# Gate and up projection of an FFN: six more chunk pairs by seven products, one product of two taken over by GpSimd, and a reordered opening

## The reference, cut to what matters

```python
xn = rms_norm(x, ffn_norm_g[l])                    # x * rsqrt(mean(x^2) + eps) * g
gate, up = jnp.split(xn @ w_gate_up[l], 2, axis=-1)  # 1024 -> 2 * 2816
x = x + (jax.nn.silu(gate) * up) @ w_down[l]
```

## Time and profile before

| what | us |
|---|---|
| median of three runs | 1330.39 |
| profiled execution | 1330.17 |
| its span | 1328.5 |
| PE busy | 1303.2 (98%) |
| DVE busy | 806.3 (61%) |
| ACT busy | 575.9 (43%) |
| POOL busy | 465.6 (35%) |

### The profile page before, as it was taken

The page is one execution under the profiler, slowest core; times in us unless marked ns, Lnnn a source line. Parts: engine busy times, 40 slices in busy tenths (PEclk is TensorE's granted clock), DMA queues, the critical chain, the costliest instruction groups (busy, mean ns, idle before and its releaser), DMA issues.

```text
span 1328.5 us, 17433 instructions
## 1 busy us (share of the span) xinstructions
PE 1303.2 (98%) x6598; PEld 1088.7 (82%) x6598; DVE 806.3 (61%) x1245; ACT 575.9 (43%) x996; POOL 465.6 (35%) x210
## 2 busy tenths in 40 slices
PE   8999999999999999999999999999969999999998
PEld 6888888887878888888888888897758999998886
DVE  7998727233383366665534655578796777764443
ACT  5224333223242565666633345676443434433223
POOL 2455444444444443344444342343250000014441
PEclk9999999999999999999999999999989999999999
DMA  4233333334622422324333363433213333222321
GB/s 162 93 95 119 111 94 96 95 94 144 223 87 72 142 79 64 96 66 189 122 101 96 103 194 102 128 113 127 79 39 120 98 117 105 96 95 96 109 90 72
DMA packets 43260, 143.54 MB, mean 108 GB/s; under 512 B 6033, under 2 KB 6033, under 8 KB 42417
## 3 DMA queue, kind: packets, MB, share of 16 engines
q1 hardware_dynamic: 39376, 129.88, 30.8%
q10 hardware_dynamic: 3808, 12.64, 2.6%
HBM read 121.46 MB, written 10.49 MB: 99 GB/s over the span
## 4 chain that ended last, share of the span: by engine, by line
PE 92%; DVE 4%; ACT 2%; POOL 1%; DMA 1%; issue 1%; SPq 0%; DVEq 0%; ACTq 0%
PE bank L1875 29%; PE bank L1877 29%; PE bank L1876 29%; PE bank L2045 2%; POOL w_lo L618 1%; PE bank L2034 1%; PE bank L2035 1%; DVE xs L1684 1%; PE bank L1899 1%; ACT w_hi L686 0%; DMA x<-x_in 0%; DVE pool_sqsum L1185 0%; DVE xs L1690 0%; ACT pool_xg L712 0%; PE bank L2190 0%
## 5 line engine op out<-in xcount | busy, mean ns | idle before, releaser
L618 POOL TENSOR_TENSOR w_lo<-raw,w_hi 128x1024 fp32r<-128x1024 f32 (+1 forms) x148 | 371.2, 2511 | 567.3 <-ACT w_hi L686 567.2
L686 ACT ACTIVATE w_hi<-raw 128x1024 fp32r<-128x1024 f32 x149 | 156.2, 1054 | 230.6 <-PE bank L1877 181.8
L663 POOL TENSOR_TENSOR w_lo<-raw,w_hi 128x1024 fp32r<-128x1024 f32 x22 | 53.7, 2443 | 253.7 <-ACT w_hi L1090 253.7
L1875 PE MATMUL bank<-y_hi,w_hi 128*128 128x512 f32 x256 | 101.5, 396 | 0.0
L1876 PE MATMUL bank<-y_lo,w_hi 128*128 128x512 f32 x256 | 101.2, 396 | 0.0
L1877 PE MATMUL bank<-y_hi,w_lo 128*128 128x512 f32 x256 | 101.2, 395 | 0.0
L1875 PE MATMUL bank<-pool_xg,w_hi 128*128 128x512 f32 x248 | 98.4, 397 | 0.0
L1876 PE MATMUL bank<-pool_xg,w_hi 128*128 128x512 f32 x248 | 98.1, 396 | 0.0
L1877 PE MATMUL bank<-pool_xg,w_lo 128*128 128x512 f32 x248 | 98.1, 395 | 0.0
L1841 DVE TENSOR_TENSOR act<-acts,act 128x512 fp32r<-128x512 f32 x22 | 55.2, 2515 | 58.1 <-ACT act L1096 58.1
L1200 DVE TENSOR_TENSOR x<-bank,x 128x512 f32<-128x512 f32 x16 | 11.1, 692 | 118.4 <-PE bank L1877 115.3
(11 more groups left out here) (418 smaller groups left out, 3614.8 us busy)
## 6 DMA issues: line engine op xcount, KB each, us to landing
raw<-stream SPq DMA_DIRECT2D x187, 512.0 KB, 3.5
raw_x<-stream SPq DMA_DIRECT2D x18, 512.0 KB, 4.3
spill<-x ACTq DMA_DIRECT2D x2, 2048.0 KB, 7.3
xg_spill<-mla_xg ACTq DMA_DIRECT2D x2, 2048.0 KB, 11.9
rope_q<-turned_hl SPq DMA_DIRECT2D x64, 64.0 KB, 2.2
zx<-xg_spill SPq DMA_DIRECT2D x2, 1536.0 KB, 9.6
stacked<-fq SPq DMA_DIRECT2D x24, 128.0 KB
stacked<-fk SPq DMA_DIRECT2D x24, 128.0 KB
```

Source lines behind the costliest of these rows:

```text
L618: pool.tensor_tensor(w_lo[:, j % RING, 0:width], raw[:, j % RAW, 0:width], plain(w_hi[:, j % RING, 0:width]), ALU.subtract).then_inc(tile_ ...
L663: pool.tensor_tensor(w_lo[:, s, 0:D], raw[:, d % RAW, 0:D], plain(w_hi[:, s, 0:D]), ALU.subtract).then_inc(tile_lo, 1)
L686: act.activation(w_hi[:, t % RING, 0:width], raw[:, t % RAW, 0:width], ACT.Copy).then_inc(tile_hi, 1)
L1875: pe.matmul(target, a_hi, b_hi, start=start, stop=False)
```

## The change

Five edits, all in the FFN.

1. `PLAN` makes all 18 pairs from 4 to 21 "S".
2. gate*up of these pairs (`finish`, DVE) is removed; POOL makes it, in a loop of 18 instructions that stands behind its last front tile and ahead of its first down tile.
3. ACT multiplies x by the norm weights into xs (8 instructions ahead of the norm's root), and DVE multiplies by `inv` in 4 instructions of 128 x 1024 in place of 8 of 128 x 512.
4. ACT's splits of front tiles 4, 6 and 7 move ahead of the root, of three of the `scaled_high` and of `front_silu(1)`; DVE's `front_evacuate(1)` and `front_gate(1)` move behind the first two and three differences.
5. The sixth product (a22) goes to the first half of bank 0 in place of the second half of bank 1, and waits for one combining addition in place of four; the seventh waits for three.

```diff
-PLAN = "N" * FRONT + "SSN" * 6
+PLAN = "N" * FRONT + "S" * 18
...
             low_tiles(FIRST_OPERAND, first=TILE["mix"] + 24)
+            pool.wait_ge(act_ready, FRONT)
+            for p in range(FRONT, FC):
+                pool.wait_ge(gate_silu, p + 1)
+                pool.wait_ge(combined, COMBINED * (SEVENS.index(p) + 1))
+                pool.tensor_tensor(acts[:, p, :], acts[:, p, :], gated[:, p % 2, :], ALU.mult).then_inc(act_ready, 1)
             pool.wait_ge(tile_lo, DOWN)
...
             split_tile("ffn_up", 0, 0)
+            for k in range(DC):
+                act.activation(xs[:, k, :], x[:, k, :], ACT.Copy, scale=col("ffn_norm", k)).then_inc(n.xg_hi, 1)
+            split_tile("ffn_up", 0, 1)
             norm_root(norm["ffn"])
-            split_tile("ffn_up", 0, 1)
             front_silu(0)
             split_tile("ffn_up", 0, 2)
-            for i in range(DC // 2):
+            scaled_high(0)
+            split_tile("ffn_up", 0, 3)
+            for i in range(1, DC // 2):
                 scaled_high(i)
+            split_tile("ffn_up", 0, 4)
             front_silu(1)
-            split_tile("ffn_up", 0, 3)
-            split_tile("ffn_up", 0, 4)
...
-            def scaled(k):
-
-                dve.scalar_tensor_tensor(xs[:, k, :], x[:, k, :], col("ffn_norm", k), inv[:], ALU.mult, ALU.mult).then_inc(n.x_ready, 1)
+            def scaled(i):
+
+                c = xs[:, 2 * i:2 * i + 2, :]
+                dve.wait_ge(n.xg_hi, n.chunks + DC + 2 * i + 2)
+                dve.tensor_tensor(c, c, inv[:].unsqueeze(1).to_broadcast([P, 2, S]), ALU.mult).then_inc(n.x_ready, 1)
...
-            def finish(p):
-
-                dve.wait_ge(gate_silu, p + 1)
-                up = acts[:, p, :] if PLAN[p] == "S" else pair_banks(p)[1][:]
-                dve.tensor_tensor(acts[:, p, :], up, gated[:, p % 2, :], ALU.mult).then_inc(act_ready, 1)
...
             front_evacuate(0)
-            for c in range(DC):
-                scaled(c)
+            for i in range(DC // 2):
+                scaled(i)
             front_gate(0)
             for i in range(DC // 2):
                 scaled_low(i)
-            front_evacuate(1)
             dve.wait_ge(n.xg_lo, n.chunks + DC + DC // 2)
...
             dve.tensor_tensor(b12, b22, b12, ALU.subtract).then_inc(n.x_ready, 1)
-            front_gate(1)
+            front_evacuate(1)
...
             t_low(0)
+            front_gate(1)
...
                 if p == FRONT:
                     front_gate(p - 1)
-                else:
-                    finish(p - 1)
...
-                pe.wait_ge(combined, COMBINED * i + 4)
-                half_product(banks[1][:, second], p, "a22", *t_split("t4"), True, True)
+                pe.wait_ge(combined, COMBINED * i + 1)
+                half_product(banks[0][:, first], p, "a22", *t_split("t4"), True, True)
+                pe.wait_ge(combined, COMBINED * i + 3)
                 half_product(banks[2][:, second], p, "s4", *scaled_part(1, 1), True, True)
```

More of the change, by code:

```diff
@@ L1044, in scaled_high @@
             def scaled_high(i):
-                act.wait_ge(n.x_ready, DC + 2 * i + 2)
+                act.wait_ge(n.x_ready, DC + i + 1)
                 act.activation(xs_hi[:, 2 * i:2 * i + 2, :], xs[:, 2 * i:2 * i + 2, :], ACT.Copy).then_inc(n.xg_hi, 1)
             def t_high(i):
-                act.wait_ge(n.x_ready, 2 * DC + i + 1)
+                act.wait_ge(n.x_ready, DC + DC // 2 + i + 1)
                 source = xs[:, CHUNKS[(0, 0, 1, 1)[i]], TOKENS[(0, 1, 1, 0)[i]]]
@@ L1680, in front_gate @@
                 dve.tensor_tensor(acts[:, p, :], acts[:, p, :], front_gated[:, p % 2, :], ALU.mult).then_inc(act_ready, 1)
-            def scaled(k):
-                dve.scalar_tensor_tensor(xs[:, k, :], x[:, k, :], col("ffn_norm", k), inv[:], ALU.mult, ALU.mult).then_inc(n.x_ready, 1)
+            def scaled(i):
+                c = xs[:, 2 * i:2 * i + 2, :]
+                dve.wait_ge(n.xg_hi, n.chunks + DC + 2 * i + 2)
+                dve.tensor_tensor(c, c, inv[:].unsqueeze(1).to_broadcast([P, 2, S]), ALU.mult).then_inc(n.x_ready, 1)
             def scaled_low(i):
                 c = slice(2 * i, 2 * i + 2)
-                dve.wait_ge(n.xg_hi, n.chunks + DC + i + 1)
+                dve.wait_ge(n.xg_hi, n.chunks + 2 * DC + i + 1)
                 dve.tensor_tensor(xs_lo[:, c, :], xs[:, c, :], plain(xs_hi[:, c, :]), ALU.subtract).then_inc(n.xg_lo, 1)
@@ L1694, in t_low @@
             def t_low(i):
-                dve.wait_ge(n.xg_hi, n.chunks + DC + DC // 2 + i + 1)
+                dve.wait_ge(n.xg_hi, n.chunks + 2 * DC + DC // 2 + i + 1)
                 dve.tensor_tensor(t_lo[:, i], (b11, b12, b22, b21)[i], plain(t_hi[:, i]), ALU.subtract).then_inc(n.xg_lo, 1)
@@ L1752, in combine_up @@
             def combine_up(p):
-                combine(p, "a22", acts[:, p, TOKENS[0]], pair_banks(p)[1][:, TOKENS[1]], u3_sum)
+                combine(p, "a22", acts[:, p, TOKENS[0]], pair_banks(p)[0][:, TOKENS[0]], u3_sum)
             def combine_gate(p):
                 combine(p, "s4", gated[:, p % 2, TOKENS[1]], pair_banks(p)[2][:, TOKENS[1]], v_sum)
+            T_READY = DC + DC // 2
             front_evacuate(0)
-            for c in range(DC):
-                scaled(c)
+            for i in range(DC // 2):
+                scaled(i)
             front_gate(0)
@@ L1765, in _ @@
                 scaled_low(i)
-            front_evacuate(1)
             dve.wait_ge(n.xg_lo, n.chunks + DC + DC // 2)
-            dve.wait_ge(n.x_ready, 2 * DC)
+            dve.wait_ge(n.x_ready, T_READY)
             dve.tensor_tensor(b11, b12, b11, ALU.subtract).then_inc(n.x_ready, 1)
             dve.tensor_tensor(b12, b22, b12, ALU.subtract).then_inc(n.x_ready, 1)
-            front_gate(1)
-            dve.wait_ge(n.x_ready, 2 * DC + 2)
+            front_evacuate(1)
+            dve.wait_ge(n.x_ready, T_READY + 2)
             dve.tensor_tensor(b22, b22, b11, ALU.subtract).then_inc(n.x_ready, 1)
             t_low(0)
-            dve.wait_ge(n.x_ready, 2 * DC + 3)
+            front_gate(1)
+            dve.wait_ge(n.x_ready, T_READY + 3)
             dve.tensor_tensor(b21, b21, b22, ALU.subtract).then_inc(n.x_ready, 1)
@@ L1846, in _ @@
             act_low(1)
-            finish(FC - 1)
             for d in range(2, FC):
```

## The result

| what | before | after |
|---|---|---|
| median | 1331.09 (5 runs, 1330.19 to 1333.2) | 1338.20 (5 runs, 1338.17 to 1338.83) |
| ratio after/before, 95% interval | | 1.0053 [1.0039, 1.0067] |
| profiled execution, span | 1330.17, 1328.5 | 1338.83, 1337.1 |

The kernel before was run again beside the changed one, hence its five runs. The interval lies above 1.002: slower, by 7.1 us in the medians and 8.7 in the profiled executions. Lines of the changed kernel stand 0 to 10 higher than in the kernel before (L618 is the same, L1703 is L1713). First the page of the changed kernel: its busy times, TensorE's row of slices, the chain that ended last by engine, and the group of GpSimd's products.

The account below looks back on a forecast made before the run. The prediction took PE's matmuls to bound the kernel before, and DVE's turn to set the pairs' pace after the change. 1330.17 - 5 (opening) + 8.3 (pairs) + 10 (end) = 1343.5 us, range 1327 to 1348.

Parts of the forecast that it names:

- The opening: Up to pair 4's third product: DVE sets the pace, 1005.3 against 1011.55; 5 us less, bounds 3 and 8.
- The half clock that was reckoned with behind the third product: Pair 4: PE stands about 5 us before its third product, so the clock falls again, up to 3.0 us.
- The pairs: Pairs 5 to 21: POOL's product holds DVE 1.25 us, turn 10.9 against PE's 9.91; 8.3 us more.
- the first of the signs: Pairs: POOL's 18 products start about 0.5 to 1 us after the silu's end and last 1.3 to 1.9.
- DVE-bound, it gives nothing: The sixth product's cell in the pairs: its dropped wait gives nothing if DVE-bound, at PE's pace at most 1.
- The sum: Whole kernel: 1330.17 - 5 + 8.3 + 10 = 1343.5 us.
- The end: Ahead of the down projection: PE idle 7.0 us, then half clock costing 3.0; 10 us more, bounds 7 and 11.
- The half clock behind it: Behind the pause ahead of the down projection: the clock falls to half and costs 3.0 us once more.
- A: Rival, pairs: POOL waits for PSUM readers and blocks 0.5, turn 10.1 to 10.2; 1331.5 us; chance 0.22.
- B: Rival: pairs run at PE's pace, -7.5, POOL never costs a turn; kernel faster, 1325.0 us; chance 0.13.
- C: Rival: the opening gives nothing, half clock twice and POOL's three tiles eat it; 1348.5 us; chance 0.10.

Follow-up runs that it names:

- e2: The kernel before with the reordered opening (edits 3 and 4) alone: 1324.56 us, ratio 0.9955.
- e8: The changed kernel with the old opening (edits 3 and 4 undone, the other three kept): 1343.18 us, ratio 1.0088.
- e11: e7 with `front_evacuate(1)` put back ahead of the first two differences on DVE: 1319.68 us, ratio 0.9914.
- e4: The changed kernel with GpSimd multiplying only 8 of the 512 columns of gate*up, the other 504 left out: 1325.66 us, ratio 0.9964.
- e5: The changed kernel with GpSimd's product of pair p also waiting for DVE's low part of s2 of pair p+2: 1326.22 us, ratio 0.9966.
- e9: The changed kernel with edit 5 alone undone (sixth product in its old cell with its old wait): 1344.26 us, ratio 1.0100.
- e10: e7 with the sixth product in its old cell and its old wait: 1320.97 us, ratio 0.9925.
- e3: The changed kernel with the low part of down tile 0 ahead of GpSimd's last product: 1331.75 us, ratio 1.0008.
- e7: The changed kernel with the edits of e5 and e3 together: 1319.63 us, ratio 0.9915.

## Why the prediction was right, point by point

**The opening, -5 forecast, -4.5 found.** Right as to place and size: DVE reached pair 4's first sum at 996.23 (995.8 forecast; 0.5 of the difference is that its stretch began at 965.62 and not at 965.11) and PE stood 3.07 before tile 6 (3.5) and 3.67 before the third product (5). The half clock that was reckoned with behind the third product came too and cost 2.6; net of the stall that is gone, 1.2 were lost up to pair 5. e2 and e8 give 6.0 and 5.0 for the opening by itself. e11 shows that it is DVE's stretch.

**The pairs, +8.3 forecast, +5.0 found.** The mechanism was right: GpSimd asks in the second sum, takes the next boundary, holds the low part of a11, and the copy carries the delay to PE; e4 and e5 take only the overlap away and the 16 waits vanish. The sizes: the block is 1.10, not 1.25, since a part of GpSimd's 1.74 lies beside DVE's sum, and pair 5 still ran at PE's pace (9.91). The two take off 4; pair 21, which lasted 10.8 and not the 9.9 I gave it, since PE still waits for its copy, puts 0.9 back. Nor is the first of the signs there as I wrote it: GpSimd's products start 0.08 behind the silu's end, for the profile counts the wait for DVE's boundary in their own 1.74.

"DVE-bound, it gives nothing" of the sixth product's cell was the step that failed: e9 puts it at 6.1 us, e10 at 1.2 at PE's pace. I had asked which of two waits PE meets first, and not where the fourth addition stands once DVE's turn is stretched: at 1087.60 to 1088.02 with the change, 1.1 behind the sixth product's start at 1086.90. The sum wasn't hurt, for its turn of 10.9 came from DVE's row alone and so already was the turn of a kernel without that wait.

**The end, +10 forecast, +8.1 found.** The pause was forecast link by link at 7.0 and is 6.7; e3 takes 4.85 of it away by moving one instruction. The half clock behind it cost 1.4, not 3.0, and this is the term that was mis-sized: I took the price from the kernel before, where 6.00 us at half clock followed a gap of 11.60; here some 3 us followed one of 6.41. The price was also a little high where I took it: the 14 matmuls of the earlier trace rows take 3.3 us at the full pitch of 0.23, so 2.7 and not 3.0 were lost there.

**The sum.** Two of the three terms were too high, the pairs by 3.3 and the end by 1.9; the opening was 0.5 too favourable. So 13.3 were forecast for the 8.6 of the profiled executions and the 7.1 of the medians. Sign and places were right; the size was one and a half to nearly two times what came.

**The rivals.** A said that GpSimd waits for PSUM readers, as its tile of 10.80 seemed to the earlier trace rows: in the pairs it didn't, it started at the first boundary, and e5's turn had to be made by a wait. The Trainium skill, "SBUF — State Buffer", section "Who interferes with whom", says that a VectorE instruction contends with GpSimd where it has two SBUF inputs, not where it has at most one (outside its 2-port modes), and that whichever of the two issues first keeps the shared port for its whole instruction. The rows of the pairs agree, and so does e5's free place beside PSUM readers. The two long tiles of the old opening do not: in e8 the tile is asked for at 984.56, seven DVE instructions with two SBUF inputs start behind that, and the tile's end, by PE's start at 995.51, fits a start at DVE's first PSUM reader (993.07). There A's reading holds. B was right that 9.91 is there to be had, but under an order that the change doesn't have (e7). C was wrong on the opening.

## What to carry to other kernels

Before work is moved from VectorE to GpSimd, find the instruction of VectorE beside which it will run: here the same product cost 1.10, 0.6 or 0 us by its moment, while doing it on VectorE costs 0.60. A wait dropped from a producer should be priced where its releaser stands after the change, not before. And the last unit of a pipelined loop needs its own count: what was hidden behind work that the change removes comes out whole, here as a pause of 6.7 us, 4.9 of them by one instruction's place in a queue.

## What the hardware showed unexpectedly

- GpSimd's 128x512 product is 1.26 to 1.30 us where nothing holds it up and 1.74 when asked for 0.5 us before VectorE's next boundary; it waits out the running instruction and not the next. But with the old opening a 128x1024 tile loses one boundary after another between VectorE's instructions, in two kernels (10.80 us before; e8, where two take 13.58). What sets the two apart was not tried and is open.
- VectorE's instructions with one PSUM and one SBUF input ran at 0.42 beside GpSimd's product as without it (e5).
- After the 6.7 us pause TensorE had 0.54 of its clock for 3.15 us and then all of it; after e5's pause, 6.41 by its last wait too, it had 0.50 for the first 3.07 us and 0.81 over the next 3.00:

```profile
1189.43:1192.50 3.07, 3.07 (x12) 2.67 (x13) 0.00 (x0) 0.00 (x0) 2.27 (x1) 0.50 0.46 171
1192.50:1195.50 3.00, 3.00 (x16) 2.45 (x16) 1.18 (x1) 1.70 (x3) 1.65 (x1) 0.81 0.48 175
```

The lower level is 1.2 of 2.4 GHz. Nearly the same pause was followed by 19 matmuls in the second stretch in one kernel and by 16 in the other, some 0.5 us. In the pairs of the changed kernel, with a stall of some 0.5 us in each turn, the clock stayed at 1.00; behind the stall of 3.67 us in pair 4 it was 0.58 over 7.07 us.
